# A hybrid encoder step on one core: state rows, bias rows and the scan's time steps made in the feature projection

## What is computed

```python
q, k, v, z, xbc, dt_raw, u, vc = split_cols(x @ w_in, IN_SIZES)
# A: band attention, 6 heads x 64; own 64 rows and the 512 before them
s = einsum(q, k) * 64**-0.5 + table[:, clip(rel, -63, 128) + 63]
o_a = softmax(s) @ v
# B: state space scan, 6 heads x 64, chunks of 128 rows
xbc, conv_state = causal_dwconv(xbc, conv_prev, conv_w, conv_b)   # width 4; the last 3 rows are an output
dt = softplus(dt_raw + dt_bias);  a = -exp(a_log)
acum = cumsum(dt * a)             # in each chunk
# used: exp(acum_i - acum_j), exp(acum_last - acum), exp(acum), exp(acum_last)
# C: u * (tril(w_s) @ vc + b_s); then norms, output projection, a feed-forward part
```

## Time and profile before

| | |
|---|---|
| median of 3 runs | 2809.88 us (2809.85 to 2812.94) |
| the profiled execution's own time | 2820.15 us |
| its span, first to last instruction | 2818.7 us |
| mean granted clock of PE | 0.957 |
| PE busy | 2577.7 us, 91% |
| DVE busy | 1638.2 us, 58% |
| ACT busy | 1053.8 us, 37% |
| POOL busy | 168.8 us, 6% |
| stage project_features, first to last instruction and stores | 291.7 to 642.5 |
| stage attention | 642.5 to 914.6 |
| stage ssd_and_gmlp | from 914.6 |

### The profile page before, as it was taken

The page is one execution under the profiler, slowest core; times in us unless marked ns, Lnnn a source line. Parts: engine busy times, 40 slices in busy tenths (PEclk is TensorE's granted clock), DMA queues, the critical chain, the costliest instruction groups (busy, mean ns, idle before and its releaser), DMA issues. The chain is left out here.

```text
span 2818.7 us, 47061 instructions
## 1 busy us (share of the span) xinstructions
PE 2577.7 (91%) x15094; PEld 2363.7 (84%) x15094; DVE 1638.2 (58%) x3296; ACT 1053.8 (37%) x1996; POOL 168.8 (6%) x244
## 2 busy tenths in 40 slices
PE   6999799965998787995999989999999979999998
PEld 5888699964997776884899989999999967888885
DVE  5342445433775776665899986667766654333333
ACT  4444322214663113222555554445555442111110
POOL 0000100001000570110000000000000000000000
PEclk9999899987997898997999999999999989999999
DMA  5443623157441545444777779777788744322321
GB/s 198 137 156 118 207 97 101 66 50 176 118 126 38 169 140 199 161 159 155 256 245 245 243 252 292 257 258 250 239 257 255 245 165 145 94 77 78 93 78 52
DMA packets 418766, 468.52 MB, mean 166 GB/s; under 512 B 45309, under 2 KB 352389, under 8 KB 418651
## 3 DMA queue, kind: packets, MB, share of 16 engines
q1 hardware_dynamic: 405210, 418.50, 48.5%
q0 software_dynamic: 13456, 48.76, 5.2%
HBM read 312.51 MB, written 155.60 MB: 166 GB/s over the span
## 5 line engine op out<-in xcount | busy, mean ns | idle before, releaser
L2265 PE MATMUL fu_ps_a<-fu_x_hi,fu_w 128*128 128x354 f32 (+1 forms) x1056 | 348.2, 330 | 45.3 <-ACT fu_part L2042 16.9
L2267 PE MATMUL fu_ps_a<-fu_x_hi,fu_w 128*128 128x354 f32 (+1 forms) x1056 | 346.4, 328 | 0.0
L2266 PE MATMUL fu_ps_a<-fu_x_lo,fu_w 128*128 128x354 f32 (+1 forms) x1056 | 345.8, 328 | 0.0
L107 PE MATMUL fd_ps_y<-fd_w_hi,fd_h_hi 128*128 128x512 f32 (+1 forms) x748 | 292.5, 391 | 17.6 <-DVE fd_h_lo L2454 17.6
L108 PE MATMUL fd_ps_y<-fd_w_lo,fd_h_hi 128*128 128x512 f32 (+1 forms) x748 | 291.9, 390 | 0.0
L109 PE MATMUL fd_ps_y<-fd_w_hi,fd_h_lo 128*128 128x512 f32 (+1 forms) x748 | 291.6, 390 | 0.0
L2454 DVE TENSOR_TENSOR fd_h_lo<-fd_h_raw,fd_h_hi 128x256 fp32r<-128x256 f32 (+1 forms) x187 | 77.7, 417 | 311.6 <-ACT fd_h_hi L2426 311.6
L2265 PEld LDWEIGHTS fu_ps_a<-fu_x_hi,fu_w 128*128 128x128 f32 x1056 | 201.1, 190 | 53.5 <-ACT fu_part L2042 18.0
L107 PE MATMUL pf_ps_y<-pf_xt_hi,pf_w_hi 128*128 128x304 f32 (+1 forms) x728 | 221.2, 304 | 20.8 <-DVE pf_xt_lo L581 18.7
L2426 ACT CAST fd_h_hi<-fd_h_raw 128x256 fp32r<-128x256 f32 (+1 forms) x187 | 74.7, 401 | 404.8 <-PE fd_ps_y L109 394.2
L109 PE MATMUL pf_ps_y<-pf_xt_hi,pf_w_lo 128*128 128x304 f32 (+1 forms) x728 | 220.9, 303 | 0.0
(11 more groups left out here) (318 smaller groups left out, 5803.6 us busy)
## 6 DMA issues: line engine op xcount, KB each, us to landing
fu_w<-fu_w_split SPq DMA_DIRECT2D x176, 512.0 KB, 4.4
fu_w_raw<-ffn_w_in SPq DMA_DIRECT2D x132, 512.0 KB, 5.5
fu_w_split<-fu_w SPq DMA_DIRECT2D x44, 1024.0 KB, 4.6
fd_h_raw<-h_t SPq DMA_DIRECT2D x176, 128.0 KB, 2.2
h_t<-fu_val SPq DMA_DIRECT2D x88, 176.0 KB, 1.9
fd_raw<-ffn_w_out SPq DMA_DIRECT2D x22, 512.0 KB, 4.7
x_rows<-pr_xr SPq DMA_DIRECT2D x16, 512.0 KB, 2.8
xt<-pr_xt SPq DMA_DIRECT2D x16, 512.0 KB, 4.0
```

The source lines that it names most:

```text
L107: pe.matmul(out, lhs_hi, rhs_hi, start=first, stop=False)
L2265: pe.matmul(out, wh, xh, start=first and k == 0, stop=False, skip_group_check=True)
L2266: pe.matmul(out, wh, xl, start=False, stop=False, skip_group_check=True)
L2267: last = pe.matmul(out, wl, xh, start=False, stop=k == KH - 1, skip_group_check=True)
```

## The change

It does three things.

Convolution states as rows: `taps`, `shift` and the sample's state come in with three DMAs as 56 rows of 128 numbers (`vec_rows`); PE transposes them in front of its first product, DVE copies them to `vecs`. At the stage's end PE transposes `halo` and `halo_smp` (each 128 x 21), ACT copies them to `states_t`, SP stores 21 rows of 512 bytes with each of two DMAs.

Bias laid out by query: POOL's store of `ext` writes, instead of 6 rows, for each head and each query its own 640 columns (768 rows of 2560 bytes) to `bias_rows`. In attention ACT issues one DMA from there straight into `bias`; `flip`, `bias_up`, the twelve products with `flip` and the six copies are gone.

Time steps, sums and decays: the preparation moves from ssd_and_gmlp into project_features. Loads go to POOL at the stage's start; DVE's chain (21 instructions) and two exponentials of ACT come between groups 1 and 2 (`then`); the two matmuls, the sums and the three other exponentials come behind the last group. The tiles stay in SBUF through attention. In ssd_and_gmlp chunk 0's front no longer waits for a preparation; PE still transposes `ws` and DVE masks it, which PE now waits for before its first use of `ps_off`. `gb` and `st_in` load behind chunk 0's three loads.

```diff
 def project_features(nc, d):
+    steps = {name: nc.alloc_sbuf_tensor(f"dt_{name}", [P, NC_, HEADS], F32) for name in ("dt", "dta", "ncum", "ecum", "dts", "etot")}
...
-        def groups(eng, step):
+        def groups(eng, step, then=None):
             step(0, 0, 0)
             step(1, 1, 0)
+            if then:
+                then()
...
-                sp.wait_ge(conv_done, NXBC * (NG + 1))
-                for c in range(3):
-                    sp.dma_start(d["prompt_ssm_conv"][c].rearrange("(m p) -> p m", p=P), halo[:, :, c], allow_slow_non_contiguous=True).then_inc(state_stored, 16)
-                for c in range(3):
-                    sp.dma_start(d["sample_ssm_conv"][c].rearrange("(m p) -> p m", p=P), halo_smp[:, :, c], allow_slow_non_contiguous=True).then_inc(state_stored, 16)
-                sp.wait_ge(state_stored, 16 * 6)
+                sp.wait_ge(states_done, 2)
+                sp.dma_start(d["prompt_ssm_conv"].rearrange("c (m p) -> (c m) p", p=P), states_t[:, 0, :]).then_inc(state_stored, 16)
+                sp.dma_start(d["sample_ssm_conv"].rearrange("c (m p) -> (c m) p", p=P), states_t[:, 1, :]).then_inc(state_stored, 16)
+                sp.wait_ge(state_stored, 32)
...
-                for c in range(4):
-                    pool.dma_start(taps[:, :, c], d["ssm_conv_w"][c].rearrange("(m p) -> p m", p=P),
-                                   allow_slow_non_contiguous=True).then_inc(small_loaded, 16)
-                pool.dma_start(shift[:], d["ssm_conv_b"].rearrange("(m p) -> p m", p=P), allow_slow_non_contiguous=True).then_inc(small_loaded, 16)
-                for c in range(3):
-                    pool.dma_start(halo_smp[:, :, c], d["state_ssm_conv"][c].rearrange("(m p) -> p m", p=P),
-                                   allow_slow_non_contiguous=True).then_inc(small_loaded, 16)
+                pool.dma_start(vec_rows[0:4 * NXBC, :], d["ssm_conv_w"].rearrange("c (m p) -> (c m) p", p=P)).then_inc(vec_loaded, 16)
+                pool.dma_start(vec_rows[4 * NXBC:5 * NXBC, :], d["ssm_conv_b"].rearrange("(m p) -> m p", p=P)).then_inc(vec_loaded, 16)
+                pool.dma_start(vec_rows[5 * NXBC:, :], d["state_ssm_conv"].rearrange("c (m p) -> (c m) p", p=P)).then_inc(vec_loaded, 16)
+                make_identity(pool, ident, zero_done, ident_done)
+                pool.dma_start(dt[:, 0:NT, :], d["dt_rows"][0:SEQ, :].rearrange("(t p) h -> p t h", p=P)).then_inc(dt_loaded, 16)
+                pool.dma_start(dt[:NSMP, NT, :], d["dt_rows"][SEQ:ROWS, :]).then_inc(dt_loaded, 16)
+                pool.dma_start(dt_bias[:], bc_row(d["ssm_dt_bias"], HEADS)).then_inc(dt_loaded, 16)
+                pool.dma_start(a_row[:], bc_row(d["ssm_a_log"], HEADS)).then_inc(dt_loaded, 16)
...
-                pool.dma_start(d["rel_ext"], ext[:]).then_inc(ext_stored, 16)
+                by_query = bass.AP(ext[:].tensor, ext[:].offset + P - 1, [list(ext[:].ap[0]), [-1, P], [1, WIN]])
+                pool.dma_start(d["bias_rows"], by_query).then_inc(ext_stored, 16)
                 pool.wait_ge(ext_stored, 16)
...
-                groups(act, step)
+                def exponents():
+                    act.wait_ge(dt_loaded, 64)
+                    act.activation(a_row[:], a_row[:], ACT.Exp).then_inc(exp_done, 1)
+                    act.wait_ge(chain_done, 3)
+                    act.activation(ex[:], ex[:], ACT.Exp).then_inc(exp_done, 1)
+                groups(act, step, exponents)
+                act.wait_ge(ncum_done, 2)
+                act.activation(ecum[:], ncum[:], ACT.Exp, scale=-1.0)
+                act.activation(etot[:], ps_y[:, 6, P:P + NC_ * HEADS].rearrange("p (t h) -> p t h", h=HEADS), ACT.Exp)
+                act.activation(den[:], num[:], ACT.Exp).then_inc(exp_done, 1)
+                act.wait_ge(states_turned, 1)
+                for e in range(2):
+                    act.copy(states_t[:, e, :], ps_y[0:3 * NXBC, 7, e * P:(e + 1) * P]).then_inc(states_done, 1)
...
+                    if k == 0:
+                        dve.wait_ge(vec_turned, 1)
+                        dve.tensor_copy(vecs[:].rearrange("p a b -> p (a b)"), ps_y[:, 7, 0:NV]).then_inc(vec_done, 1)
...
-                groups(dve, step)
+                groups(dve, step, time_steps)
+                dve.wait_ge(cum_done, 1)
+                dve.tensor_scalar(ncum[:], ps_y[:, 6, 0:NC_ * HEADS].rearrange("p (t h) -> p t h", h=HEADS), -1.0, None,
+                                  ALU.mult).then_inc(ncum_done, 1)
...
+                pe.wait_ge(ident_done, 1)
+                pe.wait_ge(vec_loaded, 48)
+                pe.transpose(ps_y[:, 7, 0:NV], vec_rows[:], ident[0:NV, 0:NV]).then_inc(vec_turned, 1)
...
                             for j in range(8):
+                                if k == 0 and j == 7:
+                                    pe.wait_ge(vec_done, 1)
...
+                pe.wait_ge(conv_done, NXBC * (NG + 1))
+                pe.wait_ge(const_done, 1)
+                pe.wait_ge(dta_all_done, 1)
+                flat = dta[:].rearrange("p t h -> p (t h)")
+                pe.matmul(ps_y[:, 6, 0:NC_ * HEADS], upper[:], flat, start=True, stop=True)
+                pe.matmul(ps_y[:, 6, P:P + NC_ * HEADS], ones[:], flat, start=True, stop=True).then_inc(cum_done, 1)
+                for e, rows in enumerate((halo[:].rearrange("p a b -> p (a b)"), halo_smp.rearrange("p a b -> p (a b)"))):
+                    last = pe.transpose(ps_y[0:3 * NXBC, 7, e * P:(e + 1) * P], rows, ident[:])
+                last.then_inc(states_turned, 1)
 def attention(nc, d):
-                toeplitz = bass.AP(d["rel_ext"].tensor, 0, [[1, P], [WIN + P, HEADS], [1, WIN]])
-                sp.dma_start(bias_up[:], toeplitz).then_inc(bias_loaded, 16)
...
-                pool.wait_ge(bias_copied, HEADS)
+                pool.wait_ge(ident_done, 1)
+                pool.wait_ge(bias_loaded, 16)
...
-                for h in range(HEADS):
-                    act.wait_ge(bias_flipped, h + 1)
-                    act.copy(bias[:, h, :], (ps_s[:, 0] if h % 2 == 0 else ps_t)[:, 0:WIN]).then_inc(bias_copied, 1)
+                act.dma_start(bias[:], d["bias_rows"].rearrange("h p c -> p h c")).then_inc(bias_loaded, 16)
...
-                for h in range(HEADS):
-                    wait_if(pe, bias_copied, h - 1)
-                    dst = ps_s[:, 0] if h % 2 == 0 else ps_t
-                    pe.matmul(dst[:, 0:512], flip[:], bias_up[:, h, 0:512], start=True, stop=True)
-                    pe.matmul(dst[:, 512:WIN], flip[:], bias_up[:, h, 512:], start=True, stop=True).then_inc(bias_flipped, 1)
-                pe.wait_ge(bias_copied, HEADS)
 def ssd_and_gmlp(nc, d):
...
-                for t in range(4):
+                load(0, 0)
+                sp.dma_start(gb[:], d["gmlp_b"].rearrange("g i -> i g"), allow_slow_non_contiguous=True).then_inc(small_loaded, 16)
+                sp.dma_start(st_in[:], d["state_ssm"].rearrange("(m p) n -> p m n", p=P)).then_inc(small_loaded, 16)
+                for t in range(1, 4):
                     load(t, t)
...
-                pool.wait_ge(prep_done, 1)
+                pool.wait_ge(small_loaded, 64)
...
-                    if isinstance(t, int) and t == 0:
-                        pe.wait_ge(prep_done, 1)
...
                     wait_if(pe, y1_done, t)
+                    if isinstance(t, int) and t == 0:
+                        pe.wait_ge(wt_done, 1)
```

More of the change, by code:

```diff
@@ L383, in project_features @@
         W = 2 * AW + XBC
+        dt, dta, ncum, ecum, dts, etot = (steps[name] for name in ("dt", "dta", "ncum", "ecum", "dts", "etot"))
+        dt_bias, a_row = m.sb("dt_bias", [P, HEADS]), m.sb("a_row", [P, HEADS])
+        raw_at = m.here()
         w_raw = m.sb("w_raw", [P, 4, W])
+        ex, w2, num, den = (m.over(name, raw_at + 512 * i, [P, NC_, HEADS]) for i, name in enumerate(("ex", "w2", "num", "den")))
+        ones, upper = m.over("ones", raw_at + 2048, [P, P]), m.over("upper", raw_at + 2560, [P, P])
+        states_t = m.over("states_t", raw_at + 3072, [3 * NXBC, 2, P])
         w_hi, w_lo = m.sb("w_hi", [P, KD, W], F32R), m.sb("w_lo", [P, KD, W], F32R)
@@ L513, in step @@
                         load_xt(g + 2, p)
+                pool.wait_ge(w_lo_done, KD)
+                pool.memset(ones[:], 1.0).then_inc(zero_done, 1)
+                pool.wait_ge(zero_done, 2)
+                pool.affine_select(out=upper[:], in_=ones[:], compare_op=ALU.is_ge, fill=0.0, base=0,
+                                   pattern=[[1, P]], channel_multiplier=-1).then_inc(const_done, 1)
                 step(0, 0, 0)
@@ L707, in attention @@
         cache = m.sb("cache", [P, 4, HEADS, 2, HD])
-        bias, bias_up = m.sb("bias", [P, HEADS, WIN]), m.sb("bias_up", [P, HEADS, WIN])
-        ident, flip, ident_r = m.sb("ident", [P, P]), m.sb("flip", [P, P]), m.sb("ident_r", [P, HD], F32R)
+        bias = m.sb("bias", [P, HEADS, WIN])
+        ident, ident_r = m.sb("ident", [P, P]), m.sb("ident_r", [P, HD], F32R)
```

(7 more changed lines are left out.)

143 lines of the change are left out of this document (59 added, 84 removed).

## The result

The changed kernel takes 2830.31 us (median of 7, 2820.55 to 2837.91), the kernel before 2810.16 us beside it on the same chip (median of 7). The ratio is 1.006, with a 95% interval of 1.004 to 1.008. It is **slower**, by 20 us in the medians (0.6%, clear of the interval), where the forecast was 2777.2 us and faster.

The account below looks back on a forecast made before the run. It took PE to bound project_features, then transfer queues and waits between stages. Gains 22.6 + 2.5 + 8.4 less 0.3 and 0.5 made 32.7 us, giving 2777.2 us (range 2770 to 2785).

Parts of the forecast that it names:

- D: Work added where PE is busy in project_features: first product 0.3 us late, bias store 0.5 (0 to 2), time steps nothing.
- The bound below, 8.4: Bias store in project_features: at least 8.4 us, the time of the same amount read over 128 partitions.
- The bound above, 21: Bias store in project_features: 21 us if only six of 16 engines carry it, at 92 GB/s.
- Rival (3): Bias store goes through one engine: at 80 us 27 lost, at 130 us 77 lost (2854); chance 0.04, half of it slower.
- For 35 us nothing waits: Bias store's cover: group 2's `xt` load behind it on POOL must start by 367; beyond that ACT is late.
- A: End of project_features: six DMAs of 4-byte elements removed, attention starts 22.6 us earlier (20.5 to 23).
- rival (4): State stores stay slow because landing, not pieces, was their cost: end-of-project_features gain only 2, 2798 us; chance 0.02.
- C: Start of ssd_and_gmlp: the preparation before chunk 0's transposes falls away, 8.4 us less (7.3 to 9.2).
- B: Start of attention: flips and copies removed, DVE starts 4.2 us earlier, of which 2.5 us stay (0 to 5).
- rival (1): Attention's start gains nothing or less, as the cache's loads delay tiles 0 and 1; total gain 29 to 30, 2780.5; chance 0.18.
- D's other two terms: In project_features: first product 0.3 us late (0 to 0.5, or 2); time steps between groups 1 and 2 cost nothing.
- rival (2): Time steps hold DVE and ACT over nine microseconds, or table changes recur each pass; price 3 to 8, 2783; chance 0.12.

Follow-up runs that it names:

- 48 partitions: Changed kernel, but `ext` goes to DRAM, returns as eight shifted copies per head, and the bias is stored from 48 partitions; 2784.39 us, ratio 0.989.
- the second: Changed kernel with the bias store made twice, the second time into another DRAM tensor; 2883.73 us, ratio 1.026.
- the bias undone: Changed kernel with the bias made as before (18 KB stored, `bias_up`, flips and copies back), states and time steps still changed; 2784.58 us, ratio 0.990.
- DRAM to DRAM: Changed kernel, but `ext` goes to DRAM first and a second DMA lays the bias rows out from there, six heads outermost; 2784.32 us, ratio 0.989.

## Why the prediction was wrong

**The step that failed** is in D: "Meanwhile stores of q and k share the engines, and ACT waits for them; I put 0.5 (0 to 2)", on a store that was to take 8.4 to 21 us. The term measured 44 us (PE's waits for ACT: 46.2 against 2.1). Two things went wrong in it.

First the duration: 58.4 us. The bound below, 8.4, was taken from `at_bias_up`, as large and with pieces as many, but with 128 partitions on the SBUF side (and a load, not a store). The bound above, 21, let six engines work at the speed of engines with a good source. That held for a DRAM source (18.6) and not for six partitions. Rival (3) had the right kind of event, a store that outlasts its cover, and was priced from one engine. It was then dismissed with the row of `at_bias_up`, which has the same pieces and another source. The runs put the cause at the narrow source: from 6, 12 and 48 partitions the same bytes took 58.4, 30.6 and 14.7 us. Another queue (57.3 us) and all 16 engines (69.8 us) didn't make it faster. That it is groups of four partitions which share a way out of 22 to 24 GB/s fits these durations (with eight to a way for the 48) and the step at half time, and was not tested by itself.

Second the cover. "For 35 us nothing waits" looked at what is queued behind the store on POOL, the load of `xt`. That was true. But the store also lies beside others on the DMA engines. The stores of `qk_hi` and `qk_lo` have two buffers each, and ACT can't write the third before the first has landed. So the cover is that of the double buffers. A store of 14.7 us cost PE nothing (2.2 us of waits against 2.1), one of 30.6 some 10 (12.4), one of 58.4 cost 44, and the second its full 51. By these the cover is some 14 to 20 us long, an estimate, as the two shorter stores also began later and went over more engines. The sentence that priced it named the right wait, but gave it a size without asking how long a q store is late when the engines that it needs are held. At the 21 us of the bound even this cover would have cost only 1 to 7 us; at 58.4 it costs 44.

**A was right in mechanism and slightly small.** The last convolution to attention's start went from 29.3 to 5.6 us, 23.7 less, against 22.6. The chain went as worked out: PE's sums and DVE's two steps beside ACT's change of function (1.28 us, and its exponential begins 0.02 after it), then the copies, then the stores, with 2.4 us from the second issue to the next stage. The 1.38 us of drain that the Trainium skill adds (ScalarE: Activation LUTs, What ACT_TABLE_LOAD costs) does not show in this row either. Stored by element again, the states cost 25.3 us in the median, which rules out rival (4): the pieces were the cost.

**C was right.** The first chunk's transposes came 7.7 us sooner after the stage's start (8.4 forecast; `st_in` landed 5.6 us after its issue at 929.88, by PE's release at 935.47, beyond the bound of 5.3), and the stage is shorter by 7.3 us from its start to the first product of the one behind it (158.4 to 151.1).

**B went as rival (1)**, nearly. DVE's first bias came at +15.7 (14.9 forecast). PE's waits for tiles moved forward to tile 1: 31.6 us in all, with the 19.2 of the start. From attention's start to the turning of the cache the changed kernel takes 201.5 us (664.6 to 866.0) against 204.2 (642.5 to 846.7). That is 2.7 gained; but with the bias undone it takes 203.7, with DRAM to DRAM 202.7 and with 48 partitions 199.8. So B gives 1 to 4 in the traces, and the medians can't tell it from nothing (2784.6 for the bias undone, 2784.3 and 2784.4 for the other two). The reason given for rival (1) was right: the cache's loads, issued 10.4 us after the stage's start instead of 18.9, lie before tiles 1 and 2; put behind tiles 1 and 2, they gave 9.2 us in the trace.

The rest of attention shows a difference that is none of the change's. In the profiled execution of before, the 20 us that follow the turning of the cache ran with a granted clock of 0.64 on the mean, so that PE was for most of it at the lower of its two levels (1.2 GHz). PE had worked 6.13 us of the 9.3 ahead of that. In the changed kernel it had worked 6.83 of 10.0, and the clock stayed up. First before, then after, beginning with the turning:

```profile
846.70:856.00 9.30, 6.13 (x35) 4.87 (x35) 4.71 (x9) 4.60 (x9) 0.00 (x0) 0.85 0.04 9
856.00:876.00 20.00, 20.00 (x110) 19.15 (x109) 10.20 (x34) 8.02 (x18) 0.54 (x1) 0.64 0.18 45
```

```profile
866.00:876.00 10.00, 6.83 (x49) 5.58 (x50) 5.68 (x12) 5.64 (x11) 0.00 (x0) 1.00 0.08 17
876.00:896.00 20.00, 20.00 (x167) 19.29 (x166) 15.72 (x52) 11.87 (x26) 1.08 (x2) 1.00 0.20 55
```

PE got 110 matmuls through in 20 us where it now did 167. From the turning to the next stage this makes 67.9 us before and 60.7 after. The storing from 48 partitions showed the same drop (68.2 us), the bias undone did not (60.6). Nor did the states stored by element (863 to 883 us), at a granted clock of 1.00 although PE had worked the same 6.13 of 9.3 us ahead of it. So the drop comes and goes with the same program of attention, and is no part of the change. At 7.2 us it would account for most of the 10 us by which the profiled execution of before lies above its median.

**D's other two terms** went well. The first product came at 300.2, 1.5 earlier. Between groups 1 and 2 DVE's chain and ACT's two changes of function ran, from DVE's first step at 443.9 to its last at 452, and PE had no wait there: rival (2) did not come.

**The account.** ACT's last copy out of the projection's products (`cin`) comes at 655.94 instead of 610.26, 45.7 later, of which 44.1 are PE's waits. Less A 23.7, B 2.7 and C 7.3 that makes 12.0 us slower. The spans differ by 5.7 and, with the 7.2 of the clock taken out of before's, by 12.9. The medians differ by 20.2. The profiled execution of after lies 4.4 us under its median (its runs are 2820.6 to 2837.9); what the longer ones do more, no trace here shows.

Without the bias part the sum was close: A, C and the first product were to give 22.6 + 8.4 - 0.3 = 30.7 us, and with the bias undone the medians give 28.0, with PE waiting 4.8 us for ACT instead of 2.1. With the rows by query from DRAM they give 28.7, where all terms without the failed one come to 33.2; of the 4.5 us that are missing, B accounts for 1 in that trace (1.5 instead of 2.5), and no row here for the rest.

## What to carry to other kernels

Price a DMA by how its SBUF side is spread over partitions, and not only by its bytes, pieces and engines. A row with as many partitions on that side is a bound; one with 128 is none for six. Then look for its cover in two places, what is queued behind it, and what else goes through the DMA engines meanwhile and how many buffers that has; the slack is the smallest of them. When a price per piece comes out of two runs, look into the trace whether the rate is constant: here a step in it told that the unit was wrong. And a load that is early is not free while others are late: move it behind them by its place in the queue and not by a wait, for a wait also holds all that stands behind it.

## What the runs showed of the hardware

- A store of 768 pieces of 2560 bytes out of SBUF took 58.4 us from 6 partitions, 30.6 from 12 and 14.7 from 48. From DRAM, with the same six outermost, it took 18.6. It didn't matter whether a software queue (58.4 us) or a hardware queue (57.3 us) carried it.
- From six partitions it moved 47 GB/s, and 24 after half the time; made twice at once, 51 and 24 with twice the engines' time. This fits groups of four partitions that share some 22 to 24 GB/s, an estimate from these rows.
- Sixteen engines sent to six such partitions were busy 95.6% of the time and moved 27 GB/s; the store took 69.8 us. A busy share near 1 at so few GB/s means engines that wait, here for a source; the 93% at 10 GB/s came with 4-byte pieces.
- The pairs of 152 KB stores beside the six-partition store, on another queue, were complete after a median of 21.7 us instead of about 2, though 64% of the engines' time was free on the mean. That would fit stores that are spread over all engines and done only when the slowest is; it was not tried by itself.
